# Finer steps for the projections that run beside the token mixers of a hybrid decoder layer

## The chip, the cores and the metric

The kernel runs on one core of a Trainium2 chip. TensorE multiplies matrices, VectorE and ScalarE work element by element, GpSimd (POOL) does a few side jobs, and SyncE (SP) issues the DMAs. Each engine works through its own list of instructions in order and waits on semaphores for the others. The metric is the device time of one launch in microseconds (us).

## The reference

One layer, 1024 tokens, width 1024, everything in float32:

```python
h = rms_norm(x, ln_mix)
(fq, fk, fv, ff, sz, sxbc, sdt, gq, gk, gv, ga, gr, hq, hf, hi, hg) = split_columns(h @ w_in, IN_SPLITS)
y_fox  = forgetting_attention(fq, fk, fv, ff + fox_f_bias, ...)   # causal softmax attention, 4 heads of 64, decaying
y_ssd  = mamba2_mixer(sz, sxbc, sdt, ...)   # causal convolution (4 taps) + silu, then a scan in chunks of 128
y_gla  = gla_mixer(gq, gk, gv, ga, gr, ...)           # gated linear attention, chunks of 64
y_hgrn = hgrn2_mixer(hq, hf, hi, hg, ...)             # the same recurrence, chunks of 16
x = x + concatenate([y_fox, y_ssd, y_gla, y_hgrn]) @ w_out
x = x + memory_cross_attention(rms_norm(x), rms_norm(mem), ...)   # keys and values: mem_n @ xa_wkv
x = x + conv_glu_ffn(rms_norm(x), ...)
```

## The kernel before, in words

The whole kernel is one core's program: a mixers block (about the first 771 us), then a tail block with the output projection, the cross attention and the feed-forward part. The change is in the mixers block alone.

**Projections.** `h` lies transposed in fast memory as a high and a low part (HH and HL). A weight item is 128 columns of `w_in`, 27 of them. ScalarE makes its high part (`hi`, L432), VectorE its low part (`lo`, L739), and TensorE multiplies it with the two halves of the tokens. Such a half (`halves`, L1042 in the tensor program) is eight steps over the contraction; a step is three matmuls of 128x512 (L99, L100, L101: high by high, high by low, low by high). Two PSUM banks, `gb`, take the halves in turn, and ScalarE evicts them (`copy_out`, L444). After the 27 items come 16 memory items of the cross attention's keys and values (`kv`), each four groups of three matmuls; ScalarE evicts their banks after every fourth item (`kv_out`, L458).

**The order is written out by hand.** The mixers (HGRN2, FoX, SSD, GLA, in this order) hold TensorE with small matmuls and with waits for other engines; the projections of the next mixer are dealt out in between. Tables at the top of the file, made by `spread`, give the halves for each place: in FoX one half in each of the six rounds of norms (`FOX_PRE`) and one in each of the units 4, 9, 14, 20, 25 and 30 (`FOX_UNIT`); in SSD 2, 2, 1, 1 halves at the four convolution tiles (`SSD_CONV`) and one at each of the chunks 0 to 5 (`SSD_CHUNK`). Memory items 0 to 10 run between the end of SSD and the GLA loop, none in the loop, 11 to 15 after it. The same tables are walked through by all three engines' programs: where TensorE runs a half, ScalarE's `halves` evicts the half before and, for each even one, makes the next item's high part, and VectorE's makes the low part. An engine can do nothing of its later list while it waits for such a part.

**FoX.** 32 units: two head pairs, eight query tiles, two heads. For unit n, TensorE makes scores (`scores`, L1205), VectorE logits and their maximum (`logits`, L875 to L879), ScalarE the exponential (`fox_exp`, L606), VectorE divides (`probabilities`, L884, L885). TensorE then (`outputs`) transposes the probabilities (L1219), ScalarE copies them (L617), TensorE multiplies them with the values (L1227), and ScalarE copies the result (L620). In iteration n TensorE does the scores of n + 1, then the half if there is one, then the outputs of n - 1. ScalarE does the exponential of n, the half's eviction and high part, then the copies of n - 1. VectorE does the logits of n, the low part, then the probabilities of n - 1. Before the units come the norms of q and k (`rstd` L491 and L493, `squares` L484, sums on TensorE L1074) and the copies of transposed V (L589), and two gates (L537, L754, L755).

**SSD.** Four tiles of convolution: ScalarE bias (L646), VectorE three taps (L908, L910), ScalarE tanh (L649), VectorE gate (L913), tile after tile. Then eight chunks. In chunk c TensorE does the half, the inputs of chunk c + 1 (L1256, L1261, L1266), then the products of chunk c (L1292, L1294, L1297). The inputs wait until ScalarE's two exponentials (L657, L658) and VectorE's products (L937) of chunk c have freed the banks. In the last chunks the memory tokens are normalised: statistics on ScalarE (L470), scaling on VectorE (L962), transposes on TensorE (L1280), high and low parts (L477, L969).

**GLA.** After SSD: gates, four norms, then a chain of ScalarE and VectorE over 1024 columns (L987 to L1009), and the loop of eight double chunks (L1317 to L1349).

## Time and profile before

| | us |
|---|---|
| median of 3 runs | 1868.43 |
| lowest and highest run | 1867.78, 2946.23 |
| profiled execution, its own time | 1867.99 |
| its span, first to last instruction | 1866.2 |
| TensorE matmul busy | 1731.4 (93%) |
| TensorE weight loads busy | 1374.7 (74%) |
| VectorE busy | 889.6 (48%) |
| ScalarE busy | 676.2 (36%) |

The profile's durations are those of the profiled execution. A matmul's duration holds its way through the array, so matmuls overlap; how fast TensorE gets on is read from the distance between the starts. The granted clock is given as a share of 2.4 GHz; it has the levels 1.2 and 2.4 GHz, and a value between is a mean over a stretch. A row of the timeline merges like instructions that follow each other, and ends with the idle time of the engine ahead of it and what ended that.

### The profile page before, as it was taken

To read this page: it belongs to the slowest core of one execution; us is meant where nothing else is said; L and a number is where in the kernel's file an instruction comes from. 1 tells how busy PE (TensorE), PEld (TensorE's weight loads), DVE (VectorE), ACT (ScalarE), POOL (GpSimd) and SP (SyncE) were. 2 spreads that over 40 slices of the span, in tenths; PEclk is the share of its full clock that TensorE was granted. 3 is DMA by queue.
4 is the path that set the end of the run, shared out by engine and by line. 5 is a ranking of instruction groups with operands and counts; after the bars stand their busy time and mean duration, and the time that the engine had idled before them with its cause. 6 is when DMAs were issued, how large, how long until landed. Compare 5 with 4: busy or idle time off the path is not lost.

```text
span 1866.2 us, 20863 instructions
## 1 busy us (share of the span) xinstructions
PE 1731.4 (93%) x8076; PEld 1374.7 (74%) x8076; DVE 889.6 (48%) x1487; ACT 676.2 (36%) x1218; POOL 74.2 (4%) x119
## 2 busy tenths in 40 slices
PE   6999998988888769699999999999999999999997
PEld 5787665655567546587888888888888888888886
DVE  4315584453636656545334434555543355555332
ACT  5224103633452353634434322434432334344321
POOL 2000430000001002000000000000000000000000
PEclk8999998898999899899999999999999999999999
DMA  4122000000002021350001102333323333433232
GB/s 138 45 47 46 13 12 12 23 12 12 12 23 68 12 68 57 111 194 11 14 1 46 45 29 87 94 102 91 96 74 96 101 113 98 123 92 107 85 96 96
DMA packets 166922, 121.32 MB, mean 65 GB/s; under 512 B 23448, under 2 KB 140456, under 8 KB 166824
## 3 DMA queue, kind: packets, MB, share of 16 engines
q1 hardware_dynamic: 165496, 115.53, 20.8%
q10 hardware_dynamic: 1328, 4.46, 0.7%
q8 instruction: 65, 1.06, 0.2%
q14 instruction: 33, 0.27, 0.0%
HBM read 115.77 MB, written 4.19 MB: 64 GB/s over the span
## 4 chain that ended last, share of the span: by engine, by line
PE 57%; DVE 1%; ACT 0%; DMA 0%; issue 0%; DVEq 0%
PE tail_b L99 17%; PE tail_b L101 17%; PE tail_b L100 17%; PE tail_b L2065 2%; PE tail_b L2040 1%; PE tail_b L2029 0%; PE tail_b L2052 0%; PE tail_b L1977 0%; DVE tail_wl L1741 0%; DMA tail_wr<-in_w_out 0%; PE tail_b L2184 0%; PE tail_b L2100 0%; DVE tail_xs L1776 0%; ACT tail_xs L1576 0%; DVE XR L1904 0%
## 5 line engine op out<-in xcount | busy, mean ns | idle before, releaser
L1897 DVE TENSOR_TENSOR ff_wl<-ff_wr,ff_wh 128x512 fp32r<-128x512 f32 (+1 forms) x176 | 168.5, 958 | 329.9 <-ACT ff_wh L1684 329.9
L1684 ACT ACTIVATE ff_wh<-ff_wr 128x512 fp32r<-128x512 f32 (+1 forms) x176 | 148.7, 846 | 377.9 <-PE tail_b L101 377.9
L99 PE MATMUL tail_b<-HH,ff_wh 128*128 128x512 f32 x704 | 273.9, 389 | 0.0
L100 PE MATMUL tail_b<-HL,ff_wh 128*128 128x512 f32 x704 | 273.9, 389 | 0.0
L101 PE MATMUL tail_b<-HH,ff_wl 128*128 128x512 f32 x704 | 273.9, 389 | 0.0
L99 PE MATMUL mix_gb<-HH,mix_wh 128*128 128x512 f32 x432 | 178.3, 413 | 7.7 <-ACT slots L444 3.8
L100 PE MATMUL mix_gb<-HL,mix_wh 128*128 128x512 f32 x432 | 171.5, 397 | 0.0
L101 PE MATMUL mix_gb<-HH,mix_wl 128*128 128x512 f32 x432 | 170.8, 395 | 0.0
L99 PE MATMUL tail_b<-tail_wh,HH 128*128 128x512 f32 x384 | 153.9, 401 | 10.0 <-DVE tail_wl L1741 8.8
L100 PEld LDWEIGHTS tail_b<-HL,ff_wh 128*128 128x128 f32 x704 | 132.2, 188 | 27.7
L99 PEld LDWEIGHTS tail_b<-HH,ff_wh 128*128 128x128 f32 x704 | 132.2, 188 | 27.5
L101 PEld LDWEIGHTS tail_b<-HH,ff_wl 128*128 128x128 f32 x704 | 132.2, 188 | 27.1
L101 PE MATMUL tail_b<-tail_wh,HL 128*128 128x512 f32 x384 | 150.3, 391 | 0.0
L100 PE MATMUL tail_b<-tail_wl,HH 128*128 128x512 f32 x384 | 150.2, 391 | 0.0
L739 DVE TENSOR_TENSOR mix_wl<-mix_wr,mix_wh 128x1024 fp32r<-128x1024 f32 x43 | 53.6, 1247 | 113.9 <-ACT mix_wh L432 113.3
L99 PEld LDWEIGHTS mix_gb<-HH,mix_wh 128*128 128x128 f32 x432 | 83.5, 193 | 32.5 <-ACT slots L444 5.3
L99 PE MATMUL tail_b<-ff_wh,ff_aha 128*128 128x512 f32 x256 | 100.2, 392 | 0.0
L100 PE MATMUL tail_b<-ff_wl,ff_aha 128*128 128x512 f32 x256 | 99.7, 389 | 0.0
L100 PEld LDWEIGHTS mix_gb<-HL,mix_wh 128*128 128x128 f32 x432 | 83.4, 193 | 18.6 <-issue 1.7
L101 PEld LDWEIGHTS mix_gb<-HH,mix_wl 128*128 128x128 f32 x432 | 83.0, 192 | 17.9
L99 PEld LDWEIGHTS tail_b<-tail_wh,HH 128*128 128x128 f32 x384 | 72.6, 189 | 24.8 <-issue 11.0
L101 PEld LDWEIGHTS tail_b<-tail_wh,HL 128*128 128x128 f32 x384 | 72.4, 188 | 15.6
(311 smaller groups left out, 2661.7 us busy)
## 6 DMA issues: line engine op xcount, KB each, us to landing
ff_wr<-in_ffn_w_up SPq DMA_DIRECT2D x88, 512.0 KB, 3.7
ff_wr<-in_ffn_w_down SPq DMA_DIRECT2D x88, 256.0 KB, 2.8
mix_wr<-in_w_in SPq DMA_DIRECT2D x26, 512.0 KB, 3.7
mix_wr<-in_xa_wkv SPq DMA_DIRECT2D x16, 512.0 KB, 3.7
XR<-in_x SPq DMA_DIRECT2D x8, 512.0 KB, 6.4
tail_wr<-in_w_out SPq DMA_DIRECT2D x16, 256.0 KB, 5.2
XR<-in_x ACTq DMA_DIRECT2D x1, 4096.0 KB, 18.7
tail_wr<-in_xa_wq SPq DMA_DIRECT2D x16, 256.0 KB, 4.6
```

Source lines behind the costliest of these rows:

```text
L99: pe.matmul(out, hi_w, hi_x, start=first, stop=False)
L100: pe.matmul(out, hi_w, lo_x, start=False, stop=False)
L101: return pe.matmul(out, lo_w, hi_x, start=False, stop=last)
L739: dve.tensor_tensor(WL[:, n % PART, :, :], WR[:, n % RAW, :, :], WH[:, n % PART, :, :], ALU.subtract)\
L1684: act.activation(part(FWH[m % FPART], m), part(FWR[m % FRAW], m), ACT.Copy).then_inc(w_hi, 1)
L1897: dve.tensor_tensor(part(FWL[m % FPART], m), part(FWR[m % FRAW], m), part(FWH[m % FPART], m), ALU.subtract)\
L2040: mm = pe.matmul(bank[3 + g][:, hh * N_MEM:(hh + 1) * N_MEM], QT[:, 2 * h + kk, :], ktr(2 * h + kk), start=(kk == 0), stop=(kk == 1))
L2065: mm = pe.matmul(bank3[6 + g][:, j, :], vv(m, d), PT[:, m, d // 2, :], start=(m == 0), stop=(m == 1))
```

## The change

The tables now count steps of three matmuls, and TensorE's `halves` becomes `fill`, which starts and stops inside a half. Waits for weights and banks stay at a half's first step. The other engines take their part of a half where its first step falls (`begun`), and now behind their work on the unit or the chunk. The total of steps is the same.

- FoX: 2 steps in each of the six rounds of norms; 3 in each unit, 2 where n is a multiple of four, none at 0, 16 and 32, all of them ahead of `outputs`. The place between the transposes and the products (`between`) exists and is given none. ScalarE and VectorE move eviction, high part and low part behind `fox_out` and `probabilities`.
- SSD: 9 steps at each convolution tile; in each of the chunks 0 to 4 six ahead of the next chunk's inputs and six behind them, none later. In the convolution ScalarE runs up to two tiles' bias ahead, and VectorE does the taps of tile t + 1 ahead of the gate of tile t.
- Memory: statistics and transposes one chunk earlier. Memory item 0 runs in the last SSD chunk, 1 to 6 before the GLA loop, 7 to 10 in the loop (one step ahead of the next scores and one behind in each double chunk), 11 to 15 after it.

```diff
--- before.py
+++ after.py
@@ -151,18 +151,42 @@
+def FOX_FILL(n):
+
+    return (0, 0) if n in (0, 16) else (3 if n % 4 else 2, 0) if n < 32 else (0, 0)
+
+
 _HG = spread(2 * F0, 2 * S0, [2, 2, 2, 2] + [1, 1, 1, 1, 0, 0, 0, 0])
 HG_PREP, HG_TILE = _HG[:4], _HG[4:]
-_FX = spread(2 * S0, 2 * G0, [1] * 6 + [1 if n in (4, 9, 14, 20, 25, 30) else 0 for n in range(33)])
-FOX_PRE, FOX_UNIT = _FX[:6], _FX[6:]
-_SD = spread(2 * G0, 2 * N_ITEMS, [2, 2, 1, 1] + [1] * 6 + [0] * 2)
-SSD_CONV, SSD_CHUNK = _SD[:4], _SD[4:]
+
+def in_two(spans):
+
+    return spans[0::2], spans[1::2]
+
+
+def begun(span):
+
+    return -(-span[0] // KT), -(-span[1] // KT)
+
+
+_FX = spread(2 * S0 * KT, 2 * G0 * KT, [2] * 6 + [c for n in range(33) for c in FOX_FILL(n)])
+FOX_PRE, (FOX_A, FOX_B) = _FX[:6], in_two(_FX[6:])
+_SD = spread(2 * G0 * KT, 2 * N_ITEMS * KT, [9] * 4 + [c for n in range(NT) for c in ((6, 6) if n < 5 else (0, 0))])
+SSD_CONV, (SSD_A, SSD_B) = _SD[:4], in_two(_SD[4:])
 KV_ITEMS = 4 * KT // 2
-
-
-MEM_STATS, MEM_TR = NT - 3, NT - 2
+KV_STEPS = 4
+_KV = spread(0, KV_ITEMS * KV_STEPS, [4] + [4, 4, 4, 4, 4, 4] + [c for n in range(NT) for c in (1, 1)] + [4, 8, 8])
+KV_SSD, KV_PREP, (KV_A, KV_B), KV_END = _KV[0], _KV[1:7], in_two(_KV[7:7 + 2 * NT]), _KV[7 + 2 * NT:]
+
+
+def kv_begun(span):
+
+    return -(-span[0] // KV_STEPS), -(-span[1] // KV_STEPS)
+
+
+MEM_STATS, MEM_TR = NT - 4, NT - 3
...
@@ -628,8 +652,8 @@
                     continue
                 if n < 32:
                     fox_exp(n)
-                halves(*FOX_UNIT[n])
                 fox_out(n - 1)
+                halves(*begun((FOX_A[n][0], FOX_B[n][1])))
             copy_out(2 * G0)
             act.wait_ge(E("mixed"), 1)
             act.preload_act_table_set(LN_EXP)
@@ -637,36 +661,46 @@
             act.wait_ge(E("mixed"), 2)
-            for t in range(4):
-                halves(*SSD_CONV[t])
+            conv_y = lambda t: mx(4 + t % 2)
+
+            def conv_bias(t):
                 act.wait_ge(E("half_w"), 1)
                 if t >= 2:
                     act.wait_ge(E("conv_out"), t - 1)
-                y, th = mx(4 + t % 2), data(B + 6 + t % 2)
-                act.activation(y, data(B + 2 + t), ACT.Identity, scale=CWS[:, t, 3:4], bias=CBS[:, t:t + 1])\
+                act.activation(conv_y(t), data(B + 2 + t), ACT.Identity, scale=CWS[:, t, 3:4], bias=CBS[:, t:t + 1])\
                    .then_inc(E("conv_in"), 1)
+
+            def conv_tanh(t):
                 act.wait_ge(E("conv_sum"), t + 1)
-                act.activation(th, y, ACT.Tanh).then_inc(E("conv_th"), 1)
+                act.activation(data(B + 6 + t % 2), conv_y(t), ACT.Tanh).then_inc(E("conv_th"), 1)
+
+            conv_bias(0)
+            conv_bias(1)
+            for t in range(4):
+                halves(*begun(SSD_CONV[t]))
+                conv_tanh(t)
+                if t + 2 < 4:
+                    conv_bias(t + 2)
             for c in range(NT):
-                halves(*SSD_CHUNK[c])
-                if c == MEM_TR:
-                    copy_out(2 * N_ITEMS)
                 act.wait_ge(E("s_seg"), c + 1)
                 if c >= 1:
                     act.wait_ge(E("s_upd"), c)
                 act.activation(D_, D_, ACT.Exp).then_inc(E("s_dexp"), 1)
                 act.activation(EA, M[2][:], ACT.Exp).then_inc(E("s_ea"), 1)
+                halves(*begun((SSD_A[c][0], SSD_B[c][1])))
+                if c == MEM_TR - 1:
+                    copy_out(2 * N_ITEMS)
...
@@ -888,9 +922,9 @@
                 if n < 32 and n % 16:
                     logits(n)
-                halves(*FOX_UNIT[n])
                 if n:
                     probabilities(n - 1)
+                halves(*begun((FOX_A[n][0], FOX_B[n][1])))
                 if n in (0, 16):
                     logits(n)
             norms(12, 16)
...
@@ -899,23 +933,30 @@
             dve.nop().then_inc(E("mixed"), 1)
-            for t in range(4):
-                s = B + 2 + t
-                y, th = mx(4 + t % 2), data(B + 6 + t % 2)
-                halves(*SSD_CONV[t])
+            def conv_taps(t):
+                s, y = B + 2 + t, mx(4 + t % 2)
                 dve.wait_ge(E("conv_in"), t + 1)
                 for j in (2, 1):
                     link(dve.scalar_tensor_tensor(y, SL[:, s, PAD - 3 + j:PAD - 3 + j + T], CWS[:, t, j:j + 1], y,
                                                   ALU.mult, ALU.add))
                 dve.scalar_tensor_tensor(y, SL[:, s, PAD - 3:PAD - 3 + T], CWS[:, t, 0:1], y, ALU.mult, ALU.add)\
                    .then_inc(E("conv_sum"), 1)
+
+            def conv_gate(t):
                 dve.wait_ge(E("conv_th"), t + 1)
-                dve.scalar_tensor_tensor(data(s), th, 1.0, y, ALU.add, ALU.mult).then_inc(E("conv_out"), 1)
+                dve.scalar_tensor_tensor(data(B + 2 + t), data(B + 6 + t % 2), 1.0, mx(4 + t % 2), ALU.add, ALU.mult)\
+                   .then_inc(E("conv_out"), 1)
+
+            conv_taps(0)
+            for t in range(4):
+                halves(*begun(SSD_CONV[t]))
+                if t + 1 < 4:
+                    conv_taps(t + 1)
+                conv_gate(t)
             dve.wait_ge(E("conv_out"), 4)
             S = S_SSD
             for c in range(NT):
                 sd = SCD[c % 2]
-                halves(*SSD_CHUNK[c])
                 dve.wait_ge(E("s_tr"), c + 1)
                 if c >= 1:
                     dve.wait_ge(E("s_ds"), c)
@@ -954,6 +995,7 @@
                     link(dve.tensor_tensor(S[q, hs, :], S[q, hs, :], M[5][q, 0:256].rearrange(
                         "p (h d) -> p h d", h=4)[:, hs, :], ALU.add))
                 dve.nop().then_inc(E("s_upd"), 1)
+                halves(*begun((SSD_A[c][0], SSD_B[c][1])))
                 if c == MEM_STATS:
                     dve.wait_ge(E("mem_rs"), 1)
...
             gate(2, data(B), data(B + 6), mx(2))
-            kv(1, 2)
             gate(3, data(B + 1), data(B + 7), mx(3))
+            kv(*kv_begun(KV_PREP[0]))
             norms(16, 18)
-            kv(2, 4)
+            kv(*kv_begun(KV_PREP[1]))
             norms(18, 20)
             dve.wait_ge(E("n_out"), 20)
             dve.nop().then_inc(E("mixed"), 1)
-            kv(4, 6)
...
@@ -1028,41 +1069,46 @@
                     dve.wait_ge(E("a_s"), n + 1)
                     dve.scalar_tensor_tensor(S(n + 1), S(n), ED[:, 0, n:n + 1], DM(n), ALU.mult, ALU.add)\
                        .then_inc(E("a_s"), 1)
-            kv(11, 12)
+                kv(*kv_begun((KV_A[i][0], KV_B[i][1])))
+            kv(*kv_begun(KV_END[0]))
             norms(20, 22)
-            kv(12, 14)
+            kv(*kv_begun(KV_END[1]))
             norms(22, 24)
-            kv(14, 15)
+            kv(*kv_begun(KV_END[2]))
             for p in range(2):
                 gate(4 + p, data(A + 4 + p), data(B + 6 + p), mx(4 + p))
         @block.tensor
         def _(pe):
+            def fill(s0, s1):
+                for s in range(s0, s1):
+                    m, k = divmod(s, KT)
+                    n, h = half_at(m)
+                    if k == 0 and h == 0:
+                        pe.wait_ge(E("g_lo"), n + 1)
+                    if k == 0 and m >= 2:
+                        pe.wait_ge(E("g_ev"), m - 1)
+                    mm = split_matmuls(pe, gb[m % 2][:], WH[:, n % PART, k, :], WL[:, n % PART, k, :],
+                                       half(HH[:, k, :], h), half(HL[:, k, :], h), k == 0, k == KT - 1)
+                    if k == KT - 1:
+                        mm.then_inc(E("g_mm"), 1)
+
             def halves(m0, m1):
-                for m in range(m0, m1):
-                    n, h = half_at(m)
-                    if h == 0:
+                fill(KT * m0, KT * m1)
+
+            def kv(u0, u1):
+                for u in range(u0, u1):
+                    j, (t, b) = u // KV_STEPS, divmod(u % KV_STEPS, 2)
+                    n, (c, kk) = N_ITEMS + j, divmod(j, KT // 2)
+                    k, tok = 2 * kk + b, slice(t * P, (t + 1) * P)
+                    if t == 0 and b == 0:
                         pe.wait_ge(E("g_lo"), n + 1)
-                    if m >= 2:
-                        pe.wait_ge(E("g_ev"), m - 1)
-                    for k in range(KT):
-                        mm = split_matmuls(pe, gb[m % 2][:], WH[:, n % PART, k, :], WL[:, n % PART, k, :],
-                                           half(HH[:, k, :], h), half(HL[:, k, :], h), k == 0, k == KT - 1)
-                    mm.then_inc(E("g_mm"), 1)
-
-            def kv(j0, j1):
-                for j in range(j0, j1):
-                    n, (c, kk) = N_ITEMS + j, divmod(j, KT // 2)
-                    pe.wait_ge(E("g_lo"), n + 1)
-                    if kk == 0:
-                        pe.wait_ge(E("g_ev"), 2 * (N_ITEMS + c))
-                    for t in range(2):
-                        tok = slice(t * P, (t + 1) * P)
-                        for b in range(2):
-                            k = 2 * kk + b
-                            mm = split_matmuls(pe, gb[t][:], HH[:, k, tok], HL[:, k, tok], two_rows(WH, n % PART)[:, b, :],
-                                               two_rows(WL, n % PART)[:, b, :], k == 0, k == KT - 1)
+                        if kk == 0:
+                            pe.wait_ge(E("g_ev"), 2 * (N_ITEMS + c))
+                    mm = split_matmuls(pe, gb[t][:], HH[:, k, tok], HL[:, k, tok], two_rows(WH, n % PART)[:, b, :],
+                                       two_rows(WL, n % PART)[:, b, :], k == 0, k == KT - 1)
+                    if b == 1:
                         mm.then_inc(E("g_mm"), 1)
             def norms(u0, u1):
...
@@ -1218,6 +1264,7 @@
                     for k in kb:
                         last = pe.transpose(M3[3 + m % 2][:, k % 4, :], SC[n % 3][:, k * P:(k + 1) * P], ident)
                     last.then_inc(E("p_tr"), 1)
+                fill(*between)
                 if n >= 1:
                     pe.wait_ge(E("av_ev"), n)
                 for g in range(i // 4 + 1):
@@ -1233,21 +1280,21 @@
                 if n % 16 == 0 and n < 32:
                     if n:
-                        outputs(n - 1)
+                        outputs(n - 1, FOX_B[n])
                     cum_rows(n // 16)
                     scores(n)
                     scores(n + 1)
                     continue
                 if n < 32 and (n + 1) % 16:
                     scores(n + 1)
-                halves(*FOX_UNIT[n])
-                outputs(n - 1)
+                fill(*FOX_A[n])
+                outputs(n - 1, FOX_B[n])
             norms(12, 16)
             pe.wait_ge(E("mixed"), 2)
             for t in range(4):
-                halves(*SSD_CONV[t])
+                fill(*SSD_CONV[t])
             pe.wait_ge(E("conv_out"), 4)
             def ssd_inputs(c):
                 if c >= 1:
@@ -1268,8 +1315,8 @@
             ssd_inputs(0)
             for c in range(NT):
-                halves(*SSD_CHUNK[c])
-                if c >= MEM_TR:
+                fill(*SSD_A[c])
+                if 0 <= c - MEM_TR < 2:
                     t = c - MEM_TR
                     pe.wait_ge(E("mem_sc"), t + 1)
                     pe.wait_ge(E("g_ev"), 2 * N_ITEMS)
@@ -1281,6 +1328,10 @@
                         last.then_inc(E("mem_tr"), 1)
                 if c + 1 < NT:
                     ssd_inputs(c + 1)
+                fill(*SSD_B[c])
+                if c == NT - 1:
+                    pe.wait_ge(E("mem_lo"), 4)
+                    kv(*KV_SSD)
                 pe.wait_ge(E("s_x"), 3 * c + 3)
                 pe.wait_ge(E("s_scd"), 2 * c + 2)
                 pe.wait_ge(E("s_ca"), c + 1)
@@ -1298,15 +1349,12 @@
             pe.wait_ge(E("s_upd"), NT)
             for h in range(2):
                 pe.matmul(M[h][:], WG2[:], half(data(SMALL), h), start=True, stop=True).then_inc(E("gate_mm"), 1)
-            pe.wait_ge(E("mem_lo"), 4)
-            kv(0, 2)
+            kv(*KV_PREP[0])
             norms(16, 18)
-            kv(2, 4)
+            kv(*KV_PREP[1])
             norms(18, 20)
-            kv(4, 6)
-
-
-            kv(6, 11)
+            for part in KV_PREP[2:]:
+                kv(*part)
             pe.wait_ge(E("gl_kin"), 1)
             pe.wait_ge(E("gl_kend"), 1)
@@ -1354,14 +1402,16 @@
             gla_scores(0)
             for i in range(NT):
                 gla_states(i)
+                kv(*KV_A[i])
                 if i + 1 < NT:
                     gla_scores(i + 1)
+                kv(*KV_B[i])
                 gla_outputs(i)
-            kv(11, 12)
+            kv(*KV_END[0])
             norms(20, 22)
-            kv(12, 14)
+            kv(*KV_END[1])
             norms(22, 24)
```

## Rows read from the trace of the kernel before

**Rows 1.** Busy us by engine (x instructions), then granted clock, DMA share, GB/s, by stretch.

```profile
100.00:120.00 20.00, 20.00 (x90) 16.57 (x89) 2.45 (x2) 4.29 (x6) 0.00 (x0) 1.00 0.36 54
307.00:354.00 47.00, 46.86 (x184) 34.06 (x185) 13.32 (x16) 31.88 (x54) 0.00 (x0) 0.96 0.13 34
354.00:378.00 24.00, 19.68 (x63) 10.81 (x61) 14.38 (x33) 8.92 (x24) 0.00 (x0) 0.79 0.09 22
378.00:438.00 60.00, 52.08 (x286) 36.32 (x285) 32.34 (x61) 25.56 (x58) 0.00 (x0) 1.00 0.04 10
573.00:633.00 60.00, 57.34 (x343) 46.79 (x343) 35.68 (x87) 15.92 (x27) 5.82 (x16) 0.96 0.16 53
633.00:657.00 24.00, 12.70 (x65) 8.85 (x65) 14.46 (x33) 4.17 (x8) 0.00 (x0) 0.64 0.00 1
657.00:713.00 56.00, 40.08 (x143) 28.65 (x144) 35.10 (x34) 30.46 (x36) 2.91 (x2) 0.91 0.28 92
713.00:747.00 34.00, 32.84 (x204) 19.76 (x203) 20.52 (x43) 7.59 (x17) 8.70 (x7) 0.96 0.07 20
```

**Rows 2.** Timeline of TensorE: start, us, instruction, count [idle before]; start of FoX, then iteration 12.

```profile
360.94 0.33 PE L1219 MATMUL mix_m<-ident,slots 128*128 128x128 f32 x1 [2.36 <-DVE slots L885]
...
409.99 1.77 PE L1205 MATMUL mix_m<-XR 64*128 64x512 f32 x4
411.69 0.87 PE L1219 MATMUL mix_m<-ident,slots 128*128 128x128 f32 x6
413.12 1.50 PE L1227 MATMUL mix_m<-mix_scratch,slots 128*64 128x128 f32 x12 [0.56 <-ACT mix_scratch L617]
```

**Rows 3.** Timeline of ScalarE, one round of the FoX norms: V copies, roots, squares.

```profile
316.74 0.66 ACT L589 ACTIVATE slots<-mix_m 128x256 f32<-128x256 f32 x2 [2.46 <-PE mix_m L1180]
317.82 0.69 ACT L491 ACTIVATE slots<-mix_m,eps 128x512 f32<-128x512 f32 x1 [0.42 <-PE mix_m L1074]
...
320.31 1.14 ACT L484 ACTIVATE slots<-XR 128x512 f32<-128x512 f32 x2
```

**Rows 4.** Timeline of ScalarE and VectorE: high part, low part, eviction, output copy, logits, probabilities.

```profile
313.23 1.04 ACT L432 ACTIVATE mix_wh<-mix_wr 128x1024 fp32r<-128x1024 f32 x1
...
314.31 1.23 DVE L739 TENSOR_TENSOR mix_wl<-mix_wr,mix_wh 128x1024 fp32r<-128x1024 f32 x1 [1.24 <-ACT mix_wh L432]
...
321.36 0.57 ACT L444 ACTIVATE slots<-mix_gb 128x512 f32<-128x512 f32 x1
...
402.57 1.14 DVE L875 SCALAR_TENSOR_TENSOR slots<-mix_m,mix_st,slots 128x512 f32<-128x512 f32 x2 [6.55 <-PE mix_m L1205]
...
405.13 0.62 DVE L885 TENSOR_SCALAR slots<-slots,mix_rin 128x768 f32<-128x768 f32 x1
...
410.10 0.27 ACT L620 ACTIVATE XR<-mix_m 64x128 f32<-64x128 f32 x1 [1.40 <-PE mix_m L1227]
```

**Rows 5.** Timeline of VectorE in the SSD convolution: two taps of tile 0, gate of tile 3.

```profile
541.43 2.60 DVE L908 SCALAR_TENSOR_TENSOR XR<-slots,mix_cws,XR 128x1024 f32<-128x1024 f32 x2 [5.30 <-ACT XR L646]
...
571.60 1.23 DVE L913 SCALAR_TENSOR_TENSOR slots<-slots,XR 128x1024 f32<-128x1024 f32 x1 [1.12 <-ACT slots L649]
```

**Rows 6.** Timeline of TensorE and ScalarE in the SSD chunks: inputs, products, second exponential.

```profile
619.54 1.16 PE L1261 MATMUL mix_m<-slots,ident 128*128 128x128 f32 x8 [0.85 <-ACT XR L658]
...
622.14 0.70 PE L1297 MATMUL mix_m<-slots,mix_bt 128*128 128x256 f32 x2
...
627.32 0.58 ACT L658 ACTIVATE XR<-mix_m 128x512 f32<-128x512 f32 x1
```

**Rows 7.** Timeline of VectorE, last SSD chunks: memory scaled, then its low parts, twice.

```profile
633.31 2.48 DVE L962 SCALAR_TENSOR_TENSOR slots<-slots,mix_mst,mix_scratch 128x1024 f32<-128x1024 f32 x2 [0.22 <-DVE mix_s_ssd L954]
...
646.77 1.29 DVE L969 TENSOR_TENSOR HL<-mix_gb,HH 128x512 fp32r<-128x512 f32 x2
...
657.09 1.29 DVE L969 TENSOR_TENSOR HL<-mix_gb,HH 128x512 fp32r<-128x512 f32 x2
```

**Rows 8.** Timeline of VectorE in the preparation of GLA: bias of the gate.

```profile
689.28 1.53 DVE L987 TENSOR_SCALAR slots<-mix_m,mix_bg 128x512 f32<-128x512 f32 x2
```

46 lines of the change are left out of this document (23 added, 23 removed).

## The prediction

> **What bounds the kernel now.** I read the stretches first. Where only projections run, TensorE starts 88 matmuls in 20 us, one each 0.227 us, at full clock [rows 1]. So a step of three costs 0.68 us, a half (eight steps) 5.45 us, and a memory item (four steps) 2.73 us. The same number of steps runs before and after; time can only come from TensorE's waits and half-clock stretches. These lie where little projection work stands: the first FoX units of a head pair (clock 0.79), the last two SSD chunks (0.64, 12.7 us busy of 24) and the preparation of GLA (40.1 of 56). In the FoX norms (46.9 of 47) and in the GLA loop (32.8 of 34) TensorE is the bound [rows 1].
>
> Then single FoX units. In a middle one scores start at 409.99, transposes at 411.69 right behind them, and the products at 413.12 after an idle 0.56 us for ScalarE's copy of the transposes [rows 2]; only the start of a head pair waits for the probabilities, 2.36 us [rows 2]. There is thus nothing ahead of the transposes of a middle unit for a fill to hide in, and the fill is put just there; the one wait, behind them, gets none.
>
> **FoX norms (round of two units).** Of six halves, 12 steps stay. ScalarE then sets the pace: two reciprocal roots 2.5 us, two squares 1.1, two V copies 0.7 [rows 3], 4.4 us a round; six rounds, begun 2 us into the stretch, less the last squares and two V copies, plus one eviction and one high part, end the norms at about 335. The gates (table load, two tanh, four DVE passes of 1.23) used to lie beside the last half and now stand in the open: the first transposes come at 345, not 360.94 [rows 2]. **-16 us.**
>
> **FoX units.** They take 84 steps (57.3 us) where six halves (32.7) stood. The three of the first unit, and of unit 17, go into the wait for probabilities; seen from the first transposes, 22.5 us more has to be run. Each switch between kinds of matmul adds perhaps 0.1 us, 21 more of them: +2. The small units then run at full clock: 360.94 to 378 takes 17 us, 5.45 of it projections, for work that takes some 6.4 at full clock and with the copy waits; the second pair the same, more its covered first wait. I take -14 (bounds -8 and -17), and -1 for the last unit.
>
> Against that stands a new wait. ScalarE evicts and makes the next high part, and VectorE the low part, after the previous unit's output is copied, no longer before it. Every second half (units 2, 8, 14, 20, 26) ScalarE does, from the end of the products: output copy 0.3, eviction 0.6, high part 1.05 us; VectorE, waiting in order, then the low part 1.23: ready at 3.3 us [rows 4]. Behind it are queued the next logits and probabilities, 402.57 to 405.75 in a middle unit, 3.2 us [rows 4]. TensorE needs those probabilities after scores (1.7) and fill (2.0), 3.8 us after the same point, and gets them at 6.5 to 6.8. That is 3 us each, less in the small units, 4 behind unit 14: **+15 us** in all. Now the half of 5.45 us covers these steps, since both engines do them before the outputs. The lower bound is 0, if the engines run further ahead than I read; the upper 20. The units give 22.5 + 2 - 15 + 15 = +24.5, with the norms **+8.5 us**.
>
> The engines' order bears on that: the Trainium skill, page "TensorE: Matmul & The Clock Gate", section "Architectural detail", says that ScalarE and VectorE are strict first-in-first-out, with TensorE alone reordering its weight loads. By that rule nothing gets past the waiting low part; the trace agrees, the low part at 314.31 having left VectorE idle for 1.24 us [rows 4].
>
> **SSD convolution.** Now bias, three taps, tanh and gate run as one chain per tile, and TensorE's 12 steps more end in a wait until the last gate, 571.60 + 1.23 [rows 5]. With the tiles crossed, VectorE has four times three taps at 1.3 and a gate of 1.23, 20.5 us, two low parts, and the waits of tile 2's and 3's bias for a gate. Step by step from 533.8 that ends at 563.3, where TensorE was done at 558.5. **-9.5 us**, 8.2 of it steps that moved on.
>
> **SSD chunks.** The first five chunks carry 12 steps, 8.2 us, beside 3.2 of their own and 0.4 of switches: 11.8 us each, against 9.3 with a half. The six steps ahead of the next chunk's inputs last 4.1 us. In a middle chunk the state product starts at 622.14 and the second exponential, which frees the inputs' bank, ends at 627.9 [rows 6]; even with a whole half there TensorE waited 0.85 at 619.54, when a low part stood ahead [rows 6]. With 4.1 us the inputs wait 1 us, and 2 behind each of three low parts, say +6. Then three chunks without fill instead of two. From VectorE's scaling of the memory at 633.31 two chunks take to 657.09, the second 10.3 from 646.77 [rows 7]; without its memory part of 1.29 the third takes 8.9. The scaling starts at 634.6: five chunks from 566.3 end at 631; the last eviction, table load and two squares follow. The SSD part ends at 667.3: **+10 us** with the convolution in it. The first memory item in the last chunk is hidden in its chain.
>
> **Preparation of GLA.** Six items in place of eleven. It is a chain of ScalarE and VectorE with items between. Without the high part ahead of the gates -2.2; the second pair of norms no longer stands behind two items, -5; the two low parts ahead of the gate bias, which starts at 689.28 [rows 8], are gone, -5.5; the rest of the chain keeps its order and loses the last item. The loop starts 40.5 us after the SSD's end, not 56.3: **-16 us** (bounds -10 and -19), of which 13.6 are work moved.
>
> **GLA loop.** TensorE is the bound there [rows 1], so 16 steps cost 10.9 us; one eviction of two banks stands ahead of a step, +1; switches +1.5; the half-clock end of the loop and the item behind it, now run warm, -4. **+9 us** (5 to 14). Waits for weights: the DMA of each item is issued a full item ahead as before, 0.
>
> **Sum.** 8.5 + 10 - 16 + 9 = +11.5, say +12. The profiled execution took 1867.99 us (span 1866.2), the median is 1868.43: 1880.
>
> **Rivals.**
> (a) The low part doesn't hold the next unit up. For it: VectorE has slack in a middle unit, and 6.55 us of it beside a half [rows 4]. Against: its queue is in order, and that slack lies ahead of the logits, not of the low part. Price -15: 1865. Chance 0.2.
> (b) The fills hide, in FoX too: no slower, but faster. For it: TensorE's weight loads are busy 36.3 of 60 us in the middle units against 16.6 of 20 in pure projections [rows 1]. If that room of (0.83 - 0.61) / 0.83, 27% of two stretches of 60 us, is real, the fills of the middle units vanish into it: -32 us, 1848; it decides once the starts of transposes stop following the scores directly. Against: the starts are back to back [rows 2], since narrow products load fewer columns. Chance 0.1.
> (c) The half clock. The norms would have TensorE at 3.1 of 4.4 us; at half clock a round takes 6.2, six rounds +11: 1891. For it: 0.79 and 0.64 in thin stretches; against: 0.96 in the GLA loop and 1.00 in the middle units, as full as this [rows 1]. Chance 0.12. If both it and the waits of the SSD inputs and the units come out at their upper bounds the kernel is 2% slower, over 1905.
> (d) The change only moves steps from waits to waits of the same size: 1868, in (a)'s range; 0.05.
>
> On (b): the Trainium skill, page "Perfetto Trace Analysis", section "Identifying the Most-Contended Engine", wants weight-load time, not matmul time, taken for TensorE's headroom. By that page alone the sum would be 1848; the starts in the rows weigh more.
>
> **The numbers.** The forecast, 1880 in a range of its own of 1872 to 1889, has 0.53. The range of 8 in 10 takes in (a), (c) and the bounds: 1862 to 1895. About 2%, 37 us, is what can be told from no change: faster by that 0.01, as all idle time that fills could reach would have to go; slower 0.03; within 0.96.
>
> **What would show it.** The first transposes of FoX near 345; the last output 8.5 us later than now. Waits of the FoX transposes for VectorE's probabilities, five long ones of 2 to 4 us, with the low part ahead of the logits. The inputs of SSD chunks waiting for ScalarE's exponential in chunks 1 to 4; SSD's end 10 later; the GLA loop starting 40 us after it, and taking 44. I am wrong if the long waits in FoX are missing, or if the middle units with fill last less than 2 us longer than 4.6.

## The result, and the profile after

The changed kernel took 1897.18 us (median of 4 runs, 1893.15 to 1898.24). The kernel before beside it has a median of 1879.09 over 4 runs, but one of them took 2946.23 and one 1889.74, so the comparison goes by the ratio of the undisturbed runs: 1.0143, with a 95% interval of 1.0112 to 1.0173. On another occasion (f1 below) it took 1895.71 against 1868.01, ratio 1.0133. By these ratios the change costs 25 to 27 us, and 1880 was forecast, within 1862 to 1895. The time lies above that range, by 2 us here and by 1 in f1; it is slower, but by less than 2%.

First the stretches of the changed kernel's trace that answer to [rows 1]: start and end, length, then busy us (x instructions) of TensorE, its weight loads, VectorE, ScalarE and GpSimd, then granted clock, DMA share, GB/s. In order: FoX norms, small FoX units, FoX middle units, SSD chunks with fill, the three without, preparation of GLA, GLA loop.

```profile
312.00:341.00 29.00, 24.59 (x77) 14.30 (x78) 10.24 (x13) 25.86 (x47) 0.00 (x0) 0.91 0.07 19
350.00:369.00 19.00, 15.33 (x47) 9.57 (x47) 7.56 (x20) 5.37 (x15) 0.00 (x0) 0.73 0.10 28
369.00:450.00 81.00, 66.93 (x328) 47.64 (x327) 33.38 (x62) 27.44 (x60) 0.00 (x0) 0.94 0.05 14
591.00:663.00 72.00, 62.73 (x348) 50.29 (x348) 30.64 (x74) 16.84 (x28) 4.99 (x16) 0.97 0.16 52
663.00:697.00 34.00, 23.02 (x109) 17.08 (x110) 21.12 (x49) 7.88 (x13) 0.00 (x0) 0.66 0.00 0
697.00:736.00 39.00, 25.09 (x87) 17.50 (x86) 28.86 (x29) 22.12 (x28) 1.99 (x2) 0.87 0.25 81
736.00:779.00 43.00, 42.09 (x245) 26.89 (x244) 24.19 (x45) 12.44 (x22) 8.69 (x7) 1.00 0.19 62
```

The norms and the preparation have become short, the chunks without fill have grown from 24 to 34 us at the same low clock, and the GLA loop is as full as it can be. All of this was foreseen. What was not is in the second and third rows: the small units are still at 0.73, and the middle units, which ran at 1.00 before [rows 1], have lost clock.

Stage by stage, each from one named instruction of TensorE to another (first sum of squares, first FoX transposes, last FoX products, first SSD transposes, gate product, first transposes of the GLA loop, first projection of the tail block):

```
stage                 before   after  change   predicted
up to the norms       307.1    312.3   +5.1      0
FoX norms and gates    53.8     37.4  -16.4    -16
FoX units             161.2    199.7  +38.6    +24.5
SSD convolution        50.8     41.7   -9.1     -9.5
SSD chunks to gate     84.2    105.6  +21.5    +19.5
GLA preparation        56.3     39.0  -17.2    -16
GLA loop and after     69.1     76.4   +7.3     +9
rest, with the lead   1083.8   1084.1  +0.3      0
```

The prediction gave the chunks and the convolution in one term, +10; the +19.5 is that term without its -9.5. The +5.1 ahead of the norms belongs to this one profiled execution: in the second trace of the same kernel (f1) the norms start at 305.7. From 200 to 307 us, which the change does not touch, the granted clock is 0.87 in this execution, 0.90 in f1 and 0.91 before. With its FoX units at 198.3 that trace has a span of 1891.3, 25.1 over before. The FoX units are the one stage that is far off.

Next the waits of TensorE in the FoX part of the changed kernel (312 to 560 us): instruction and what it waited for, us in total, times, longest.

```profile
PE mix_m L1274 <- ACT mix_scratch L641: 17.3, 31, 0.8
...
PE mix_m L1265 <- DVE slots L919: 9.2, 4, 4.7
PE mix_m L1251 <- DVE slots L909: 5.6, 2, 2.8
```

The first is the wait for ScalarE's copy, there before too. The others are the predicted hold, in five places, and 1.0 us at the first unit, which e5 below has too. In three of the five the transposes (L1265) wait for the probabilities, as forecast. In the other two the hold shows earlier, at the scores: they have three banks in turn, a unit of over 512 keys takes two, and the second (L1251) waits until VectorE has read the previous unit's logits out of the bank that it takes. Such a wait stands ahead of the fill. One such place in the timeline (start, us, instruction, count, idle before): ScalarE, then VectorE, then TensorE.

```profile
390.53 0.27 ACT L644 ACTIVATE XR<-mix_m 64x128 f32<-64x128 f32 x1 [1.24 <-PE mix_m L1274]
390.83 0.60 ACT L468 ACTIVATE slots<-mix_gb 128x512 f32<-128x512 f32 x1
391.32 1.05 ACT L456 ACTIVATE mix_wh<-mix_wr 128x1024 fp32r<-128x1024 f32 x1
...
392.40 1.23 DVE L773 TENSOR_TENSOR mix_wl<-mix_wr,mix_wh 128x1024 fp32r<-128x1024 f32 x1 [8.90 <-ACT mix_wh L456]
393.55 1.00 DVE L909 SCALAR_TENSOR_TENSOR slots<-mix_m,mix_st,slots 128x512 f32<-128x512 f32 x2
...
390.43 1.12 PE L1251 MATMUL mix_m<-XR 64*128 64x512 f32 x2
394.35 0.70 PE L1251 MATMUL mix_m<-XR 64*128 64x256 f32 x2 [2.80 <-DVE slots L909]
394.97 0.50 PE L99 MATMUL mix_gb<-HH,mix_wh 128*128 128x512 f32 x1
395.31 0.40 PE L100 MATMUL mix_gb<-HL,mix_wh 128*128 128x512 f32 x1
395.55 0.39 PE L101 MATMUL mix_gb<-HH,mix_wl 128*128 128x512 f32 x1
395.77 0.57 PE L99 MATMUL mix_gb<-HH,mix_wh 128*128 128x512 f32 x1
396.14 0.63 PE L100 MATMUL mix_gb<-HL,mix_wh 128*128 128x512 f32 x1
396.57 0.63 PE L101 MATMUL mix_gb<-HH,mix_wl 128*128 128x512 f32 x1
```

Output copy, eviction, high part, low part, logits: each starts as the one before it ends, as forecast, and VectorE has stood idle for 8.90 us ahead of the low part. TensorE waits 2.80 us. Then comes what the forecast did not have: a projection matmul starts 0.24 us after its predecessor at 395.55, 0.37 after it at 396.14 and 0.43 after it at 396.57. The wait is over, and the clock falls behind it. The granted clock of the stretches around the waits says the same:

```profile
390.00:402.00 12.00, 8.55 (x35) 5.71 (x34) 6.80 (x13) 4.08 (x9) 0.00 (x0) 0.86 0.16 44
434.00:450.00 16.00, 10.97 (x61) 9.21 (x60) 5.80 (x9) 5.61 (x10) 0.00 (x0) 0.79 0.13 34
470.00:486.00 16.00, 12.82 (x45) 7.76 (x45) 7.51 (x16) 4.48 (x10) 0.00 (x0) 0.79 0.12 33
509.00:521.00 12.00, 8.85 (x37) 5.88 (x36) 7.46 (x13) 4.03 (x9) 0.00 (x0) 0.86 0.17 46
```

### The profile page after: what moved, and what is told of

The parts are those of the page before. It is cut to its first block, busy times and chain, and to the rows that moved or that the text cites. A ratio compares the mean times of both kernels' runs of the same rounds, so it can differ in the third digit from the quotient of the medians.

```text
span 1896.2 us, 20864 instructions
## 1 busy us (share of the span) xinstructions
PE 1747.9 (92%) x8076; PEld 1384.2 (73%) x8076; DVE 888.1 (47%) x1487; ACT 675.2 (36%) x1218; POOL 72.5 (4%) x119
## 4 chain that ended last, share of the span: by engine, by line
PE 56%; DVE 1%; ACT 0%; DMA 0%; issue 0%; DVEq 0%
PE tail_b L99 17%; PE tail_b L100 17%; PE tail_b L101 17%; PE tail_b L2115 2%; PE tail_b L2090 1%; PE tail_b L2079 0%; PE tail_b L2102 0%; PE tail_b L2027 0%; DVE tail_wl L1791 0%; PE tail_b L2234 0%; PE tail_b L2150 0%; DMA tail_wr<-in_w_out 0%; DVE tail_xs L1826 0%; ACT tail_xs L1626 0%; DVE XR L1954 0%
## 5 line engine op out<-in xcount | busy, mean ns | idle before, releaser
L99 PE MATMUL mix_gb<-HH,mix_wh 128*128 128x512 f32 x432 | 183.2, 424 | 7.7 <-ACT slots L468 3.8
L99 PEld LDWEIGHTS tail_b<-HH,ff_wh 128*128 128x128 f32 x704 | 132.1, 188 | 27.7
L99 PEld LDWEIGHTS mix_gb<-HH,mix_wh 128*128 128x128 f32 x432 | 83.7, 194 | 43.0 <-issue 16.4
## 6 DMA issues: line engine op xcount, KB each, us to landing
XR<-in_x ACTq DMA_DIRECT2D x1, 4096.0 KB, 18.2
```

The lines of the kernel that those rows point to most:

```text
L99: pe.matmul(out, hi_w, hi_x, start=first, stop=False)
```

## The experiments

Theory: the FoX units lose time since VectorE's low part, in order ahead of the previous unit's probabilities, waits for a high part that ScalarE now makes late; the half clock behind such waits is part of their price. Two rivals: the price is that of the fills themselves, which stand where nothing waits; or the norms or the SSD chunks carry the loss. Line numbers of FoX are 1 higher in kernels with a deferred part.

**e1, FoX as before.** The rest stays changed: halves of eight steps, and both engines' parts ahead of the previous unit.

```diff
-    return (0, 0) if n in (0, 16) else (3 if n % 4 else 2, 0) if n < 32 else (0, 0)
+    return (8, 0) if n in (4, 9, 14, 20, 25, 30) else (0, 0)
-_FX = spread(2 * S0 * KT, 2 * G0 * KT, [2] * 6 + ...)
+_FX = spread(2 * S0 * KT, 2 * G0 * KT, [8] * 6 + ...)
-                fox_out(n - 1)                                  # ScalarE; VectorE alike with probabilities
                 halves(*begun((FOX_A[n][0], FOX_B[n][1])))
+                fox_out(n - 1)
```

> FoX is as before (one half in each round of norms, one in units 4, 9, 14, 20, 25, 30, high and low parts ahead of the outputs); SSD, GLA and memory items keep the change. My theory: of the 30 us that the changed kernel's span is longer, 22 arise in FoX, so the time falls by about 22 us from the changed kernel's, to 3 us or so above the kernel before; first FoX transposes to last products back at 161 us (changed 200). Rival (the fine steps cost wherever they are put, by switches and a lower clock): SSD and GLA keep half of the loss, the time stays 12 us or more above the kernel before.

1873.33 us, 1.0017 of before [0.9994, 1.0039]. FoX's units take 161.1 us again. SSD chunks still take 107.3 and the preparation of GLA 39.0. Nearly the whole loss of the change, 24 us of the medians' 28, is in FoX; SSD and GLA together come out at 4.4 us by the medians, and the interval of the ratio holds 1. That removes the SSD chunks as the place of the loss; the norms, which e1 puts back too, are removed by the table above, where they are 16.4 us shorter.

**e2, parts of the helpers one unit later.** Eviction and high part belong to the previous unit's steps and go ahead of its copies; the low part, also of the previous unit's steps, goes behind the next logits but stays ahead of the previous unit's probabilities.

```diff
...
+                halves(*begun((FOX_A[n - 1][0], FOX_B[n - 1][1])))   # ScalarE
                 fox_out(n - 1)
-                halves(*begun((FOX_A[n][0], FOX_B[n][1])))
...
+                    halves(*begun((FOX_A[n - 1][0], FOX_B[n - 1][1])))   # VectorE
                     probabilities(n - 1)
-                halves(*begun((FOX_A[n][0], FOX_B[n][1])))
```

> The changed kernel, but in FoX ScalarE's eviction and high part and VectorE's low part of a half that begins in unit n are done one unit later, ahead of its copies and of its probabilities. My theory: the five long waits of TensorE behind a low part (with the half-clock time after them some 24 us) vanish, first transposes to last products 176 to 180 us in place of 200, no TensorE wait for probabilities over 1 us but at the head pairs' starts. Rival (the low parts only show where the time goes; the fills in the units with the engines' order as it is cost it by their number): 192 us or more, the waits merely move to other units.

1885.76 us, 1.0091 [1.0056, 1.0125]; the units take 191.1, only 8.6 less than changed, where over 20 was expected. Its four runs lie far apart, 1876.96 to 1893.8. The same place in its timeline, ScalarE, VectorE, TensorE:

```profile
386.79 0.27 ACT L644 ACTIVATE XR<-mix_m 64x128 f32<-64x128 f32 x1 [1.24 <-PE mix_m L1275]
387.09 0.83 ACT L630 ACTIVATE slots<-slots,mix_nm 128x640 f32<-128x640 f32 x1
...
388.04 0.60 ACT L468 ACTIVATE slots<-mix_gb 128x512 f32<-128x512 f32 x1
388.53 1.05 ACT L456 ACTIVATE mix_wh<-mix_wr 128x1024 fp32r<-128x1024 f32 x1
...
389.61 1.23 DVE L774 TENSOR_TENSOR mix_wl<-mix_wr,mix_wh 128x1024 fp32r<-128x1024 f32 x1 [4.26 <-ACT mix_wh L456]
390.95 0.55 DVE L920 TENSOR_SCALAR slots<-slots,mix_rin 128x640 f32<-128x640 f32 x1
...
391.56 0.77 PE L1266 MATMUL mix_m<-ident,slots 128*128 128x128 f32 x5 [1.02 <-DVE slots L920]
```

The exponential is ready at 387.9, but the probabilities come only at 390.95, behind the low part. ScalarE's high part still follows the exponential, and that follows the output copy. So with ScalarE's part ahead of the copies and the low part behind the logits the waits are only shorter: `L1266 <- DVE slots L920` is 8.3 us in 6, the 1.0 of the first unit among them, and none is left at the scores.

**e3, the fill split.** The changed kernel with one step (or none) ahead of the transposes and two between transposes and products, where ScalarE's copy is waited for.

```diff
-    return (0, 0) if n in (0, 16) else (3 if n % 4 else 2, 0) if n < 32 else (0, 0)
+    return (0, 0) if n in (0, 16) else (1 if n % 4 else 0, 2) if n < 32 else (0, 0)
```

> The changed kernel, but two of each unit's three steps run between the transposes and the products (one of three ahead, none ahead where n is a multiple of four). My theory: the idle time before the products, 17.3 us in 31 waits, is covered, so first transposes to last products falls by 12 to 17 us; the five long waits stay. Rival (ScalarE's copies are delayed or the scores come late, so that the covered wait returns ahead of the next transposes): less than 5 us.

1887.5 us, 1.0101 [1.0086, 1.0116]; 9.6 less in the units (190.1), less than the 12 to 17 expected. Its waits in FoX:

```profile
PE mix_m L1265 <- DVE slots L919: 16.1, 6, 6.0
PE mix_m L1251 <- DVE slots L909: 5.6, 2, 2.8
...
PE mix_m L1274 <- ACT mix_scratch L641: 0.7, 2, 0.3
```

The copies' 17.3 us have gone to 0.7, so two steps do hide there. But 6.9 of them come back as longer waits for the probabilities, since fewer steps stand ahead of the transposes.

**e4, both.** The edits of e2 and e3 together.

> Both edits together. My theory: their gains add, since one removes waits ahead of the transposes and the other those behind them: 24 plus 14 us less than the changed kernel, so about 160 to 165 us from first transposes to last products, and a time some 10 us below the kernel before. Rival (both remove the same slack): the gain of the better one alone, 20 to 24 us.

1877.2 us, 1.0037 [0.9988, 1.0086]; units 179.9, 19.8 less than changed. It missed the 160 to 165 of the theory for the reason seen in e2: 17.8 us of waits for the probabilities are left, in seven. That is more than the 14.8 of the changed kernel, and the clock doesn't fall behind all of them. One of them, and the stretch around it:

```profile
458.26 0.55 PE L1266 MATMUL mix_m<-ident,slots 128*128 128x128 f32 x3 [2.51 <-DVE slots L920]
```

```profile
450.00:490.00 40.00, 35.91 (x169) 23.17 (x168) 19.62 (x40) 16.34 (x38) 0.00 (x0) 1.00 0.05 14
```

The projections behind this wait start 0.23 us apart. Another, of 2.54 us at 355.66, is alike. Over the whole of the units, 343 to 523 us, the granted clock is 0.94.

**e5, the low part behind the probabilities.** ScalarE as in e2; VectorE makes the low part one unit later and after the previous unit's probabilities.

```diff
                     probabilities(n - 1)
-                halves(*begun((FOX_A[n][0], FOX_B[n][1])))
+                    halves(*begun((FOX_A[n - 1][0], FOX_B[n - 1][1])))
```

> The changed kernel, but in FoX ScalarE's eviction and high part come one unit later, ahead of its copies, and VectorE's low part one unit later BEHIND its probabilities (in e2_parts_deferred it was ahead of them and five waits of 2 to 3 us stayed). My theory: what holds the next transposes is the low part standing ahead of logits or probabilities in VectorE's order, while ScalarE is held by the previous products; with the low part behind the probabilities no wait of that kind is left: first FoX transposes to last products 172 to 180 us (changed 200, e2 191). Rival (ScalarE's exponential and high part, 3 us after the last products, are the hold): 188 or more.

1868.41 us, 0.9997 [0.9985, 1.0009]: the whole loss is gone. It differs from e2 only by the place of VectorE's low part, and that is 17 us of the medians. The units take 172.5, as expected. Its waits in FoX, then VectorE and TensorE around one low part, and the clock of three stretches, the last the units as a whole:

```profile
PE mix_m L1275 <- ACT mix_scratch L641: 18.2, 32, 0.8
...
PE mix_m L1266 <- DVE slots L920: 1.0, 1, 1.0
```

```profile
377.58 0.55 DVE L920 TENSOR_SCALAR slots<-slots,mix_rin 128x640 f32<-128x640 f32 x1
381.73 1.23 DVE L774 TENSOR_TENSOR mix_wl<-mix_wr,mix_wh 128x1024 fp32r<-128x1024 f32 x1 [3.59 <-ACT mix_wh L456]
...
382.49 0.71 PE L1266 MATMUL mix_m<-ident,slots 128*128 128x128 f32 x5
```

```profile
350.00:370.00 20.00, 17.53 (x78) 11.61 (x78) 10.29 (x23) 7.96 (x21) 0.00 (x0) 1.00 0.11 27
378.00:390.00 12.00, 10.78 (x54) 7.46 (x52) 7.36 (x14) 5.33 (x12) 0.00 (x0) 1.00 0.16 44
344.00:517.00 173.00, 154.59 (x773) 106.81 (x773) 84.34 (x174) 68.40 (x160) 0.00 (x0) 1.00 0.06 16
```

The low part still waits 3.59 us, but the probabilities are through at 378.1, before it, and TensorE's transposes follow the fill directly. No new wait is left, and the clock is whole, in the small units too. In f1, the changed kernel, the same stage of 198 us has 0.93:

```profile
343.00:541.00 198.00, 166.80 (x770) 113.82 (x771) 83.66 (x173) 68.10 (x159) 0.00 (x0) 0.93 0.05 14
```

**e6, e5 with the split fill.** The edit of e3 on e5.

> e5_low_behind with two of three steps of a unit between transposes and products. My theory: the waits for the copies go too, e5's figure less 12 to 15 us, about 162 us for first transposes to last products, the time at or just below the kernel before. Rival (as in e4_deferred_split, where the low part's waits grew to 15.4 us as the copies' went): a figure within 5 us of e5.

1857.68 us, 0.9942 [0.9928, 0.9957]; units 159.4, 13 less than e5. With the order right the split pays as expected: 1.3 us of waits for copies are left of 18.2, and the waits for the probabilities grow only from 1.0 to 4.5, 2.4 of it at the first unit, which has fewer steps ahead of it now.

**e7, more steps in the norms.** On e6: 28 steps beside the norms in place of 12, the larger units get two steps in place of three.

```diff
-    return (0, 0) if n in (0, 16) else (1 if n % 4 else 0, 2) if n < 32 else (0, 0)
+    return (0, 0) if n in (0, 16) else (1 if n % 16 <= 4 else 0, 2) if n < 32 else (0, 0)
-_FX = spread(2 * S0 * KT, 2 * G0 * KT, [2] * 6 + ...)
+_FX = spread(2 * S0 * KT, 2 * G0 * KT, [4, 4, 4, 4, 4, 8] + ...)
```

> e6_low_behind_split with 28 steps in the FoX norms (4 in five rounds, 8 in the last) in place of 12, and 2 or 3 in each unit (34 in each head pair). My theory: a round of the norms is bound by ScalarE at 4.3 us with TensorE at 3.1, so two more steps a round cost little and the last four lie beside the gates: norms' first sum to first transposes 37 to 41 us (changed 37.4 in its profile), and the units 10.9 us shorter by the 16 steps; the time 7 to 11 us under e6. Rival (the norms' round grows by each step, as TensorE's own in-order work delays the sums): 48 us for the norms, no gain.

1849.68 us, 0.9897 [0.9882, 0.9912]. Norms and gates 41.1 us, units 148.0. The norms pay 3.8 us for 16 steps of 0.68 (10.9), and the units give the whole 11.4 back: the changed kernel had taken too many steps out of the norms.

**e8, SSD chunks of nine.** On e1: 43 steps in the convolution, nine per chunk in six chunks (eight ahead of the inputs, one behind; the sixth has eight), the memory's statistics and transposes a chunk later, as in the kernel before, and the first memory item behind the last chunk.

```diff
-_SD = spread(..., [9] * 4 + [c for n in range(NT) for c in ((6, 6) if n < 5 else (0, 0))])
+_SD = spread(..., [11, 11, 11, 10] + [c for n in range(NT) for c in ((8, 1) if n < 5 else (8, 0) if n < 6 else (0, 0))])
-_KV = spread(0, KV_ITEMS * KV_STEPS, [4] + [4, 4, 4, 4, 4, 4] + ...)
+_KV = spread(0, KV_ITEMS * KV_STEPS, [0] + [4, 4, 4, 8, 4, 4] + ...)
-MEM_STATS, MEM_TR = NT - 4, NT - 3
+MEM_STATS, MEM_TR = NT - 3, NT - 2
```

> e1_fox_as_before with 43 steps in the SSD convolution (36) and 53 in six chunks (8 ahead of the inputs, 1 behind; 12 in five chunks there), the memory's statistics in chunk 5 as before, and its first item in the preparation of GLA. My theory: the changed kernel's SSD is longer since five chunks hold TensorE 11.8 us while three hold nothing and are chains of 9 to 10 us. From the first SSD transposes to the SSD's end e1 takes 107.3 us; here 6 x 9.9 and two chunks, 87 to 90, with the convolution's last gate not later, and the preparation of GLA some 2 us longer: 12 to 15 us less than e1, so some 10 under the kernel before. Rival (the chunks are bound by their chain with the low part in it): 95 us or more.

1856.18 us, 0.9933 [0.9918, 0.9948], 17 less than e1. The SSD part from its first transposes to its end, e1 and then e8:

```profile
562.00:670.00 108.00, 86.56 (x457) 67.29 (x458) 52.03 (x123) 24.74 (x41) 4.96 (x16) 0.87 0.10 35
```

```profile
563.00:649.00 86.00, 72.28 (x423) 57.38 (x423) 50.18 (x120) 22.59 (x38) 5.07 (x16) 0.89 0.11 37
```

86.0 us from named instruction to named instruction in place of 107.3. Seven steps fewer are 4.8 of the 21; the rest is a third chunk without fill that is gone, and the longer fill ahead of the inputs. The edits were made at once, so their shares are not told apart. TensorE's wait for the inputs' bank, 9.4 us in six in e1, is 3.1 in four here. Some of it comes back: the stage of the convolution, with seven steps more, is 2 us longer than in e1, and the preparation of GLA, with the memory item, 3 (42.1 for 39.0).

**f1, the changed kernel again,** beside the next three.

> The changed kernel once more, on the chip and beside the runs of the kernel before that the next three share. Its profile had the HGRN2 stage, which the change does not touch, 5 us longer than the kernel before. Theory 1: that is chance of one execution (granted clock 0.87 against 0.91 there), so first norm sum at 305 to 308 us here, the span near 1890, and first FoX transposes to last products 196 to 200 us. Theory 2: it belongs to this program: 312 again.

1895.71 us, 1.0133 [1.0077, 1.019], span 1891.3. Its waits in FoX are the same to 0.1 us (9.2 in four, 5.6 in two). The 5 us ahead of the norms are not there.

**f2, all together.** FoX of e7 and SSD of e8.

> e7_more_in_norms and e8_chunks_of_nine in one kernel. Against the kernel before they were 19 and 13 us shorter, in different stages; of the second, 3 us loss of the changed SSD had been made good. If stages add: the FoX of e7 (495 us at its last products) followed by e8's convolution, chunks and GLA, which is 16 us shorter than e1's: 1830 to 1836. If the head start is lost again behind another wait: 1842 or more.

1834.75 us, 0.9805 [0.9754, 0.9856]: 33 us less than before, and 61 less than changed. Faster than before is clear; whether by 2% is not, as the interval lies on both sides of 0.98. The gains of e7 (19) and e8 (13) against before add up.

**f3, the convolution alone.** The kernel before with only the two phases; its core on VectorE:

```diff
-            for t in range(4):
-                halves(*SSD_CONV[t])   # then taps of t, gate of t
+            conv_taps(0)
+            for t in range(4):
+                halves(*SSD_CONV[t])
+                if t + 1 < 4:
+                    conv_taps(t + 1)
+                conv_gate(t)
```

> The kernel before with the convolution in two overlapping phases and nothing else (halves 2, 2, 1, 1 at its tiles as before). My theory: the wait of 6 us for the last gate (571.60 + 1.23) shrinks to under 1, TensorE's six halves of 33.5 us become the bound: first SSD transposes 5 us earlier, 1863. Rival (the chain still ends last, since the low parts stand ahead of the crossed taps): less than 2 us.

1864.06 us, 0.9958 [0.9927, 0.9988]. TensorE's wait at the end of the convolution, before:

```profile
PE mix_m L1256 <- DVE slots L913: 6.1, 1, 6.1
```

Here this wait for the last gate is gone; the one of 2.3 us ahead of the first projections is in both traces. The stage takes 44.4 us for 50.8, 6.4 less. The time is only 4 us shorter: the chunks give 2.7 more, but the preparation of GLA, which this edit doesn't touch, takes 61.2 us for 56.3, at a granted clock of 0.82 (649 to 710 us) against 0.91 [rows 1]. Why the clock is lower there stays open. So 6.4 is the convolution's own share; the 12 steps fewer in the changed kernel bring it to only -9.1, since TensorE then waits for the last gate again, 3.0 us.

**f4, eight steps in the five units that wait.** The changed kernel's order of engines, with the steps gathered to 8 in units 3, 8, 13, 19 and 24, each the unit behind one in which a high and a low part are made, and mostly 2 in the others.

```diff
-    return (0, 0) if n in (0, 16) else (3 if n % 4 else 2, 0) if n < 32 else (0, 0)
+    return ((2,3,8,2,2,2,2,8,2,2,2,2,8,2,2,0,2,2,8,2,2,2,2,8,2,2,2,1,0,0,0,0)[n - 1] if n else 0, 0)
```

> The changed kernel with its order of the engines as it is, but in FoX eight of the steps run in each unit behind one in which a high and low part is made (units 3, 8, 13, 19, 24), one to three in most others. My theory: the 3 us hold of the low part is then beside 5.5 us of steps, so TensorE has no wait for it and keeps its clock: first FoX transposes to last products 172 to 180 us, as in e5_low_behind, the time near the kernel before. Rival (e5 gained by something else than the hold, such as earlier evictions): 190 us or more.

1891.37 us, 1.0108 [1.0055, 1.0161], units 191.8. It missed the 172 to 180 expected. Waits in FoX, then one of these units on TensorE:

```profile
PE mix_m L1251 <- DVE slots L909: 8.1, 3, 2.8
...
PE mix_m L1265 <- DVE slots L919: 2.3, 3, 1.7
```

```profile
374.28 1.12 PE L1251 MATMUL mix_m<-XR 64*128 64x512 f32 x2
378.06 0.79 PE L1251 MATMUL mix_m<-XR 64*128 64x128 f32 x2 [2.65 <-DVE slots L909]
378.78 0.79 PE L99 MATMUL mix_gb<-HH,mix_wh 128*128 128x512 f32 x1
...
387.10 0.60 PE L1265 MATMUL mix_m<-ident,slots 128*128 128x128 f32 x4
```

The waits at the transposes shrink from 9.2 to 2.3 us, but three stand at the scores in place of two (8.1 us): the second piece of a unit's scores waits until VectorE has read its bank, and it stands ahead of the steps, so they can't cover it. The steps then took 8.3 us (378.78 to 387.10) where eight at full clock take 5.45. More steps at these places don't make good for the order of the helper engines; e5, with the order mended, does.

## Why the prediction was wrong

**The failed step** is the term "+15 us" for the hold by the low part, in "FoX units". As a sum of waits it was nearly exact: 14.8 us in six, of which 1.0 is the first unit's start (e5 has that too), the longest 4.7 behind unit 14 where 4 were forecast. Its price is another, because the term counted idle time alone, and TensorE's clock fell behind these waits. Changed against e5, which differs in nothing but the place of both engines' parts, it is 199.7 - 172.5 = 27.2 us of the profiles (f1: 25.8) and 1.46% of the time by the two ratios (1.0143 and 0.9997), 27 us. The remainder fits the clock within 2 us: 0.93 over the 198 us of f1 says that it was 0.07 short of full, at most 13.9 us of work not done; 13.8 of new waits and 13.9 make 27.7, for 25.8 in that trace. The same step assumed warm small units (-14): with the hold they stayed at 0.73, in e5 without it they are at 1.00. Without the hold the units cost 172.5 - 161.2 = +11.3, against 22.5 + 2 - 15 = +9.5 forecast. I had put 0 to 20 us as bounds of the hold, and 20 was too low, because they were worked out as idle time alone.

Two more pairs of runs differ in the place of the low part alone, and they show that the price of a wait is not fixed. In e2 against e5 there are 7.3 us more of waits for the probabilities (8.3 and 1.0), and the units are 18.6 longer; the granted clock is 0.94 over the 191 us of e2's. In e4 against e6 there are 13.3 more (17.8 and 4.5), and the units are 20.5 longer, at 0.94 against 0.99. So a microsecond of such waits cost 2.5 us in one pair, 1.5 in the other, and 2.0 in the changed kernel against e5.

The Trainium skill, page "TensorE: Matmul & The Clock Gate", section "Part 1: The HAM clock gate (the "warmup" mystery)", says that the throttled state is the default and that activity releases it. The traces agree in that the clock fell where TensorE had stood idle: behind the wait of 2.80 us at 394.35, in a stream that was at full clock before, the matmul step went from 0.24 to 0.43 us. They also show that not each such wait brings it, as the one of 2.51 us in e4.

**FoX norms:** right (-16.4 for -16). e7 shows however that the forecast, taking the change's split as given, left open 8 us of room there.

**Convolution and preparation:** right (-9.1 for -9.5, -17.2 for -16). f3 shows the convolution's own part, 6.4 us of its stage.

**SSD chunks:** right in kind, 2 us short (f1: 5). The inputs' waits were 8.7 us in six, 6 forecast. One of them in the trace of the changed kernel:

```profile
638.32 1.16 PE L1308 MATMUL mix_m<-slots,ident 128*128 128x128 f32 x8 [1.83 <-ACT XR L689]
```

The three chunks without fill run at 0.66, as the two did at 0.64 [rows 1].

**GLA loop:** right (+7.3 with what follows, for +9).

**Rivals.** (a), that the low part holds nothing up, is false in the changed kernel. (b), that fills hide in the middle units, is false for the place where they were put: e5 costs 11 us in the units with no wait of its own. The room was in the wait for ScalarE's copy, where e6 gets 13 us by it. (c), the half clock, gave 1891 and came nearest to the time, but by luck, since it had the wrong place: not in the norms (0.91 in the profile after, 0.96 [rows 1]), but behind the new waits. I had argued against it from the fullness of stages, which says nothing of a wait in the midst of one. (d) is false, as the time grew by 25 to 27 us.

**What stays open.** The clock's share of the 27 us is read from the traces; no run separated it from the waits, and why it falls behind some waits and not behind others as long isn't shown. Nor was it tried to put ScalarE's order back alone with the low part behind the probabilities. Why the clock is lower ahead of the norms in one execution of the changed kernel, at a cost of 5 us, wasn't looked into.

## What to carry to other kernels

When steps of a shared stream are spread, look where each helper engine does its part of it: behind the results that the bound engine needs next, not ahead. A new wait of some us in the bound engine costs more than its length when the clock falls behind it; read the granted clock of the stretch after the wait, and put more than the wait into the upper bound: in the three pairs here it cost 1.5, 2.0 and 2.5 times its length. Put the fill into a wait that the timeline shows (here the copy between transposes and products), not beside it.

## What the runs showed of the hardware

A wait of 2.80 us in a stream at full clock was enough for the half clock: matmuls 0.43 us apart for 128x512, not 0.24, from 1.4 us after the wait's end. In f4 eight steps behind a wait of 2.65 us ran 13 matmuls at the slow pace, from 378.78 to 384.5, before the spacing was 0.23 again. Over the six waits of the changed kernel, 14.8 us long, this came to about as much again. The length of the wait alone doesn't tell: in e4 the clock stayed up behind waits of 2.54 and 2.51 us (projections 0.23 us apart behind both). Waits of up to 0.8 us, 32 of them in e5, left the clock at 1.00.
